# Two transformer blocks on one core: the second half of a layer's output product in three passes of high and low parts

## The chip, the cores and the metric

The kernel runs on one core of one Trainium2 chip. The metric is the device time of one execution in microseconds (us). TensorE (PE in the profile) multiplies; VectorE (DVE) and ScalarE (ACT) do element-wise work; GpSimd (POOL) has little to do here; SyncE (SP) only issues the DMAs that bring the weights from memory. Each engine works through its own list of instructions in order, and semaphores tie the lists together.

## What is computed

A token sequence of 256 (272 with 16 meta tokens in the first block) of width 1024 goes through a first block and then through two hybrid layers. One layer of the second part is, cut to what matters here:

```python
def hybrid_layer(x, ...):
    hn = rms_norm(x, norm1_g)
    proj = jnp.einsum('bsd,df->bsf', hn, w_in)
    ya = mla_mixer(...)              # 8 heads of 64: mixed columns 0 to 511
    yb = stick_breaking_mixer(...)   # 4 heads of 64: mixed columns 512 to 767
    yc = pool_mixer(...)             # 256 mixed columns
    mixed = jnp.concatenate([ya, yb, yc], axis=-1)
    x = x + jnp.einsum('bsm,md->bsd', mixed, w_out)          # the output product
    x = x + hier_moe(rms_norm(x, norm2_g), w_group, b_group, w_expert, b_expert, w_gate, w_up, w_down)
    return x
```

`hier_moe` picks for each token one group of experts and two experts in it; the kernel streams the weights of all 32 experts.

## The kernel before

Everything is kept with features in the 128 partitions and tokens in the free dimension: `hT` is the residual as 8 tiles (index d) of 128 features, `mixT` the mixed columns as 8 tiles of 128 by 256 tokens. All arithmetic is float32. There are two ways of multiplying. A plain float32 product is one matmul in the program, which the profile shows as two records of MATMUL. A split product (`split_mm`, L1274 and after) has both operands as a high part (the value rounded to the short format fp32r, by a copy on ACT) and a low part (the rest, by a subtraction on DVE), and makes three fp32r matmuls: high by high, high by low, low by high; each is one record. The two feed-forward layers of the first block and the last units of each layer's input product use it.

Weights come as a stream of chunks of 1 MB (128 partitions by 2048 floats), one DMA each, issued by SP in `load` (L684), in a fixed order. Before each DMA SP waits until the chunk's place has been freed, and all later DMAs queue behind that wait. Six places are the slots of `ring`. In the expert stage (`moe`) 24 places are used in the order of `moe_slots` (L335): besides the ring these are pieces of `arena`, `G`, `xn`, `sq`, `sm`, `cst`, `mixT` and `hT`, each from the moment at which its old contents are dead (`slot_open`). An expert stage takes 96 chunks in 8 quads of 12, so the first two quads find all their chunks in the 24 places, and each later chunk waits for a place that an earlier quad has used.

The place of the change is in each of the two layers (index l), between the input product and the expert stage. It has three parts:

- The attention loop over 16 units (8 heads for each of two blocks of 128 queries; unit 0 to 7 has 128 keys, unit 8 to 15 has 256). The engines run it with lags, written out by `steps`. PE in step j (L1715 and after): scores of unit j (L1340), one matmul of the output product (`beside`, L1722), the turning of unit j-2's probabilities (L1351, `turn`), up to step 12 a second `beside`, and in each even step the value products of units j-4 and j-3 (L1706, `value_pair`). ACT in step s: save the turned probabilities of unit s-2 (L956, `save_T`), save the output of unit s-4 into `mixT` (L967, `save_o`), exponentials of unit s (L935). DVE in step s: weights of unit s-2 (L2137 reciprocal, L2144 scaling), maximum of unit s (L2121 and L2127).
- The output product is 4 chunks of weights with 2 rows of tiles (f) each, times 8 tiles d of the output: 64 plain products. Its mixed tiles are taken in the order 4, 5, 6, 7, 0, 1, 2, 3, since tiles 0 to 3 come out of the loop. The first 32 products (chunks 0 and 1) are the `beside` matmuls in the loop. The last 32 (chunks 2 and 3) follow the loop in `down` (L1286): chunk 2 row by row, then chunk 3 with both rows for each d, so that output tiles get finished one after another (`y_ready`).
- The residual tail: DVE adds each finished pair of tiles to `hT` (L2402), ACT squares it (L1138), DVE sums the squares (L2393 to L2397), PE makes the token sums and the router's logits (L1754 to L1763), DVE picks the experts, PE gathers their tokens (L1838), and the first quad's gate and up products begin (L1859). They free the first of the 24 places.

## Time and profile before

| | |
|---|---|
| median of 3 runs | 1188.82 us (1187.37 to 1189.06) |
| the profiled execution | 1192.25 us, its span 1190.3 us |
| PE busy | 1116.2 us, 94% of the span |
| DVE, ACT busy | 524.4 us (44%), 427.4 us (36%) |
| bytes read from memory | 321.54 MB, 273 GB/s over the span |
| mean granted TensorE clock | 0.964 |

The profiled execution lies 3.4 us above the median of the runs. All places in time that are given below are microseconds from the start of its span. Layer 0 has its loop at 635.9 to 664.8 us, its output product's second half at 664.8 to 678.8 us and its expert stage up to about 881 us; layer 1 repeats this 302 us later. A busy time of PE is the sum of modelled durations, which overlap; how fast it works is read from the starts of its instructions.

### The profile page before, as it was taken

To read this page: it belongs to the slowest core of one execution; us is meant where nothing else is said; L and a number is where in the kernel's file an instruction comes from. 1 tells how busy PE (TensorE), PEld (TensorE's weight loads), DVE (VectorE), ACT (ScalarE), POOL (GpSimd) and SP (SyncE) were. 2 spreads that over 40 slices of the span, in tenths; PEclk is the share of its full clock that TensorE was granted. 3 is DMA by queue.
4 is the path that set the end of the run, shared out by engine and by line. 5 is a ranking of instruction groups with operands and counts; after the bars stand their busy time and mean duration, and the time that the engine had idled before them with its cause. 6 is when DMAs were issued, how large, how long until landed. Compare 5 with 4: busy or idle time off the path is not lost.

```text
span 1190.3 us, 18825 instructions
## 1 busy us (share of the span) xinstructions
PE 1116.2 (94%) x7912; PEld 867.0 (73%) x7912; DVE 524.4 (44%) x998; ACT 427.4 (36%) x764; POOL 40.7 (3%) x46
## 2 busy tenths in 40 slices
PE   7999999999999999999999998997789999899776
PEld 6999999998568999999997764543359876343321
DVE  5665555885572666555685420110037543011001
ACT  5443345444372543444446420100044543011001
POOL 0000000030010000000030000000004000000000
PEclk9999999999899999999999998998989999899886
DMA  9844442462302545554368699999997879999996
GB/s 362 325 168 170 171 172 105 179 236 107 121 21 96 222 178 180 190 198 178 119 250 347 260 380 419 420 420 421 420 422 289 332 270 363 420 420 420 421 420 273
DMA packets 46058, 323.89 MB, mean 272 GB/s; under 512 B 5401, under 2 KB 5657, under 8 KB 7825
## 3 DMA queue, kind: packets, MB, share of 16 engines
q1 hardware_dynamic: 44736, 318.27, 67.8%
q0 software_dynamic: 688, 3.69, 1.0%
q8 instruction: 66, 1.08, 0.4%
q10 hardware_dynamic: 544, 0.67, 0.2%
q14 instruction: 24, 0.19, 0.0%
HBM read 321.54 MB, written 3.16 MB: 273 GB/s over the span
## 4 chain that ended last, share of the span: by engine, by line
PE 77%; DMA 14%; DVE 5%; ACT 2%; issue 2%; SPq 0%; ACTq 0%; DVEq 0%
PE bank L1276 13%; PE bank L1278 13%; PE bank L1277 13%; DMA ring<-in_stream 9%; PE bank L1859 7%; DMA sq<-in_stream 5%; PE bank L1286 4%; PE bank L1873 3%; PE bank L1838 3%; PE bank L1330 2%; PE bank L1722 2%; PE bank L1340 2%; PE bank L1887 2%; PE bank L1881 1%; PE bank L1657 1%
## 5 line engine op out<-in xcount | busy, mean ns | idle before, releaser
L1276 PE MATMUL bank<-r_hi,w_hi 128*128 128x272 f32 (+1 forms) x928 | 265.8, 286 | 0.0
L1278 PE MATMUL bank<-r_hi,w_lo 128*128 128x272 f32 (+1 forms) x928 | 265.2, 286 | 0.0
L1277 PE MATMUL bank<-r_lo,w_hi 128*128 128x272 f32 (+1 forms) x928 | 264.8, 285 | 0.0
L2011 DVE TENSOR_TENSOR w_lo<-ring,w_hi 128x2048 fp32r<-128x2048 f32 x65 | 148.9, 2292 | 129.7 <-ACT w_hi L888 129.7
L888 ACT ACTIVATE w_hi<-ring 128x2048 fp32r<-128x2048 f32 x65 | 124.5, 1917 | 206.8 <-PE bank L1278 206.8
L1276 PEld LDWEIGHTS bank<-r_hi,w_hi 128*128 128x128 f32 x928 | 175.7, 189 | 0.2
L1278 PEld LDWEIGHTS bank<-r_hi,w_lo 128*128 128x128 f32 x928 | 175.7, 189 | 0.0
L1277 PEld LDWEIGHTS bank<-r_lo,w_hi 128*128 128x128 f32 x928 | 175.4, 189 | 0.1
L2516 DVE TENSOR_TENSOR arena<-arena,bank 128x256 f32<-128x256 f32 x16 | 6.7, 421 | 224.2 <-ACT arena L1174 224.2
L1174 ACT ACTIVATE arena<-bank 128x256 f32<-128x256 f32 x16 | 6.1, 384 | 243.7 <-PE bank L1859 243.7
L1859 PE MATMUL bank<-arena 128*32 128x512 f32 x400 | 57.1, 668 | 18.8 <-DMA arena<-in_stream 10.0
L1838 PEld LDWEIGHTS bank<-rstd,arena 128*128 128x128 f32 x512 | 61.3, 200 | 14.3 <-issue 14.0
L1838 PE MATMUL bank<-rstd,arena 128*128 128x128 f32 x512 | 64.3, 286 | 0.0
L1859 PE MATMUL bank<-ring,arena 128*32 128x512 f32 x320 | 48.8, 695 | 13.9 <-DMA ring<-in_stream 13.9
L1859 PEld LDWEIGHTS bank<-arena 128*32 128x32 f32 x400 | 10.9, 115 | 54.3 <-issue 37.4
L1286 PE MATMUL bank<-mixT,ring 128*128 128x256 f32 x192 | 44.3, 393 | 0.0
L1859 PEld LDWEIGHTS bank<-ring,arena 128*32 128x32 f32 x320 | 9.9, 118 | 45.9 <-DMA ring<-in_stream 27.8
L1286 PEld LDWEIGHTS bank<-mixT,ring 128*128 128x128 f32 x192 | 37.7, 198 | 6.0 <-issue 0.6
L2521 DVE COPY G<-bank 128x512 f32<-128x512 f32 x16 | 11.1, 691 | 69.5 <-PE bank L1873 69.5
L1278 PE MATMUL bank<-hg_hi,ring_r 128*128 128x256 f32 (+1 forms) x136 | 38.6, 284 | 0.0
L1722 PE MATMUL bank<-mixT,ring 128*128 128x256 f32 x128 | 36.9, 382 | 0.0
L1278 PE MATMUL bank<-h_hi,w_lo 128*128 128x272 f32 (+1 forms) x128 | 36.4, 285 | 0.0
(376 smaller groups left out, 1970.7 us busy)
## 6 DMA issues: line engine op xcount, KB each, us to landing
ring<-in_stream SPq DMA_DIRECT2D x149, 1024.0 KB, 5.7
arena<-in_stream SPq DMA_DIRECT2D x72, 1024.0 KB, 18.7
sm<-in_stream SPq DMA_DIRECT2D x16, 1024.0 KB, 23.4
G<-in_stream SPq DMA_DIRECT2D x8, 1024.0 KB, 18.5
w_ukv<-in_stream SPq DMA_DIRECT2D x8, 1024.0 KB, 20.1
xn<-in_stream SPq DMA_DIRECT2D x8, 1024.0 KB, 21.4
sq<-in_stream SPq DMA_DIRECT2D x8, 1024.0 KB, 21.9
cst<-in_stream SPq DMA_DIRECT2D x8, 1024.0 KB, 20.3
```

The source lines that it names most:

```text
L888: copy(w_hi[:, q % 2, :], chunk((A_FFN1, A_FFN2)[f] + q), ACT.Copy).then_inc(S("w_hi_ready"), 1)
L1276: mm(dst, w_high, x_high, start=first, stop=False)
L1277: mm(dst, w_high, x_low, start=False, stop=False)
L1278: return mm(dst, w_low, x_high, start=False, stop=last)
L1286: return mm(y_half(d), w[:, f, P * d:P * d + P], src(2 * c + f), start=c == 0 and f == 0 and d % 2 == 0, stop=c == 3 and f == 1, skip_grou ...
L1330: ins = mm(bank[u - base][:, 0:T2], w[:, k, c0:c0 + P], hg2[:, k, 0:T2], start=(k == 0), stop=(k == KT - 1))
L1340: ins = mm(score_bank(u, g, m)[0:u["nq"], 0:u["L"]], lhs, rhs, start=(j == 0), stop=(j == len(parts) - 1))
L1722: ins = mm(y_half(d), down_view(A_OUT2[l] + c)[:, f, P * d:P * d + P], mixed(2 * c + f), start=n < 8 and d % 2 == 0, stop=False, skip_grou ...
L1838: ins = mm(bank[4 + half][:, P * kk:P * kk + P], x_tm[:, t, P * k:P * k + P], slots[:, s % 2, t, :], start=(t == 0), stop=(t == 1))
L1859: ins = mm(bank[6][CAP * e:CAP * e + CAP, :], xg[:, k, CAP * e:CAP * e + CAP], w[:, e, :], start=(k == 0), stop=(k == KT - 1))
L1873: ins = mm(bank[4 + half][CAP * e:CAP * e + CAP, :], hs[:, f, CAP * e:CAP * e + CAP], w[:, e, :], start=(f == 0), stop=(f == 1))
L2011: V.tensor_tensor(w_lo[:, q % 2, :], chunk((A_FFN1, A_FFN2)[f] + q), w_hi[:, q % 2, :].bitcast(F32), ALU.subtract).then_inc(S("w_lo_ready" ...
```

## The change

The second half of the output product (chunks 2 and 3) is made of split products: 96 fp32r matmuls a layer in the place of 32 plain ones. Their operands have to be split first.

- **Weights.** A half chunk (row f, 128x1024) is copied to its high part by ACT and reduced to its low part by DVE (`split_out` on both). The two halves of chunk 2 are split within the loop: ACT after the exponentials of units 10 and 12, DVE one step later, behind the maximum of units 11 and 13. The high parts of chunk 2 go into chunk 0's ring slot, those of chunk 3 into the first 2048 columns of the arena (`w_hi`), where the queries `qcat` lie, so that the halves of chunk 3 are split behind the loop. The low parts replace the weights in their own slots.
- **Mixed tiles.** For each of tiles 0 to 3, ACT copies the high part (128x256, into a piece of `G`) five steps behind the unit that completes it (`mixed_high`), and DVE makes the low part in place six steps behind it (`mixed_low`).
- **Places.** Chunk 0's ring slot is now free only when chunk 2's products are done. In `moe_slots` it moves from the 15th to the 20th place of the order.

```diff
--- before.py
+++ after.py
@@ -159,7 +159,7 @@
         hg_lo = xn_r
         sq = sb("sq", [P, 10, T1])
         rstd = sb("rstd", [P, 2, T1])
-        mixT = sb("mixT", [P, KT, T1])
+        mixT, mixT_r = both("mixT", [P, KT, T1])
         G, G_r = both("G", [P, 8, GX])
         cst = sb("cst", [P, C_ALL])
         gn = sb("gn", [P, G_ALL])
@@ -335,7 +335,7 @@
         def moe_slots(ring_slot):
 
             order = ([S_AR + 1, ring_slot[4], S_AR, ring_slot[5], S_G, S_UKV, S_XN, S_SQ, S_SM] + [S_AR + j for j in range(2, 7)]
-                     + [ring_slot[0], S_CST, S_AR + 7, S_AR + 8] + ring_slot[1:4] + [S_MIX, S_ROOT, S_HT])
+                     + [S_CST, S_AR + 7, S_AR + 8] + [ring_slot[j] for j in (1, 2, 0, 3)] + [S_MIX, S_ROOT, S_HT])
             assert sorted(order) == list(range(NS2))
             return order
 
@@ -388,10 +388,14 @@
         rows_lo = G_r[:, :, :].rearrange("p a b -> p (a b)")[:, 0:CH].rearrange("p (k n) -> p k n", k=KT)
 
         def layer_split(l, p):
-            return SPLIT_AT[1] + 3 * FC + 4 * l + p - 2 + 1
+            return SPLIT_AT[1] + 3 * FC + 8 * l + p - 2 + 1
+
+        def out_split(l, c, f):
+            return layer_split(l, 6 + 2 * (c - 2) + f)
 
         def layer_hi(p):
             return (in_hi[0], w_ukv1_r[:, :])[p % 2].rearrange("p (k n) -> p k n", k=KT)
+        mix_hi = G_r[:, :, :].rearrange("p a b -> p (a b)")[:, CH:CH + D].rearrange("p (k n) -> p k n", k=4)
         FFN_ROOT = [1, 5]
         GAINED = 4
 
@@ -584,6 +588,7 @@
             else:
                 if n == MOE_AT[l]:
                     turn, around = 0, slot_of[A_IN2[l]:A_IN2[l] + NS]
+                    last[slot_of[A_OUT2[l]]] = freed[A_OUT2[l] + 2]
                 order = moe_slots(around)
                 if n - MOE_AT[l] >= QUADS * QCH - NS2:
                     order = last_slots(order)
@@ -625,6 +630,10 @@
 
         def layer_lo(l, p):
             return ring_r[:, slot_of[A_IN2[l] + p], :].rearrange("p (k n) -> p k n", k=KT)
+
+        def out_parts(l, c, f):
+            hi = ring_r[:, slot_of[A_OUT2[l]], :] if c == 2 else w_hi[:, 0, :]
+            return tuple(v[:, D * f:D * f + D] for v in (hi, ring_r[:, slot_of[A_OUT2[l] + c], :]))
 
         def in_cols(p):
             return P if p == 2 else 256
@@ -877,6 +886,12 @@
                     act.wait_ge(S("proj_ready"), U1 + U2 * l + 2 * p - 2)
                 copy(layer_hi(p), up_view(A_IN2[l] + p), ACT.Copy).then_inc(S("w_hi_ready"), 1)
 
+            def split_out(l, c, f):
+                loaded(act, A_OUT2[l] + c)
+                name, v = freed[A_OUT2[l]] if c == 2 else ("scores_ready", SEG_M[l][1])
+                act.wait_ge(S(name), v)
+                copy(out_parts(l, c, f)[0], down_view(A_OUT2[l] + c)[:, f, :], ACT.Copy).then_inc(S("w_hi_ready"), 1)
+
             def square_unit(u, dst, src):
                 first_saved(act, u)
                 copy(dst, src, ACT.Square).then_inc(S("square_saved"), 1)
@@ -1131,7 +1146,20 @@
                             nc.scalar.activation(mixT[:, 6 + t, 0:T2], bank[3][:, T2 * t:T2 * t + T2], ACT.Copy,
                                                  scale=gain(G_PS + 2 * l + t)).then_inc(S("pool_saved"), 1)
 
-                steps(SEG_M[l], (save_T, 2), (save_o, 4), (exps, 0), (save_pool, 0))
+                def out_weights(g):
+                    if g - SEG_M[l][0] in (10, 12):
+                        split_out(l, 2, (g - SEG_M[l][0] - 10) // 2)
+
+                def mixed_high(g):
+                    n = g - SEG_M[l][0]
+                    if n >= MH and n % 2 == 1:
+                        k = (n - MH) // 2
+                        act.wait_ge(S("o_saved"), g + 1)
+                        copy(mix_hi[:, k, :], mixT[:, k, 0:T2], ACT.Copy).then_inc(S("mix_hi_ready"), 1)
+
+                steps(SEG_M[l], (save_T, 2), (save_o, 4), (exps, 0), (save_pool, 0), (out_weights, 0), (mixed_high, 5))
+                for f in range(2):
+                    split_out(l, 3, f)
                 link(copy(rs[:, 0, :], sums[:, 0, :], ACT.Sqrt))
                 for d in range(KT):
                     act.wait_ge(S("residual_ready"), 8 * (3 + 2 * l) + d + 1)
@@ -1742,7 +1770,24 @@
                     n += count
                     if j >= 4 and j % 2 == 0:
                         value_pair(g - 4)
-                down(A_OUT2[l], 2, 4, mixed, lambda k: [("o_saved", SEG_M[l][1] - 7 + 2 * (k - 4) + 1)])
+                def out_part(c, f, d, end=False):
+                    hi, lo = (v[:, P * d:P * d + P] for v in out_parts(l, c, f))
+                    x_hi, x_lo = mix_hi[:, 2 * (c - 2) + f, :], mixT_r[:, 2 * (c - 2) + f, 0:T2]
+                    mm(y_half(d), hi, x_hi, start=False, stop=False, skip_group_check=True)
+                    mm(y_half(d), hi, x_lo, start=False, stop=False, skip_group_check=True)
+                    return mm(y_half(d), lo, x_hi, start=False, stop=end, skip_group_check=True)
+
+                for c in (2, 3):
+                    for f in range(2):
+                        pe.wait_ge(S("w_lo_ready"), out_split(l, c, f))
+                        pe.wait_ge(S("mix_lo_ready"), 4 * l + 2 * (c - 2) + f + 1)
+                        for d in range(KT if c == 2 else 0):
+                            ins = out_part(c, f, d)
+                    if c == 2:
+                        ins.then_inc(S("down_used"), 1)
+                for d in range(KT):
+                    out_part(3, 0, d)
+                    out_part(3, 1, d, end=True).then_inc(S("y_ready"), 1)
                 last = l == LAYERS - 1
                 x_bank = 0 if last else 4
                 log_bank, place_bank, load_bank = (bank[4], bank[5], bank[7]) if last else (bank[0], bank[1], bank[0])
@@ -1997,6 +2042,11 @@
                 dve.wait_ge(S("w_hi_ready"), layer_split(l, p))
                 V.tensor_tensor(layer_lo(l, p), up_view(A_IN2[l] + p), layer_hi(p).bitcast(F32), ALU.subtract
                                 ).then_inc(S("w_lo_ready"), 1)
+
+            def split_out(l, c, f):
+                hi, lo = out_parts(l, c, f)
+                dve.wait_ge(S("w_hi_ready"), out_split(l, c, f))
+                V.tensor_tensor(lo, down_view(A_OUT2[l] + c)[:, f, :], hi.bitcast(F32), ALU.subtract).then_inc(S("w_lo_ready"), 1)
 
             def scale_unit(l, u):
                 dve.wait_ge(S("proj_ready"), U1 + U2 * l + u + 1)
@@ -2383,7 +2433,21 @@
                     src = bank[(15 + n) % 4].rearrange("p (a n) -> p a n", a=2)
                     link(V.tensor_copy(kcat[0:64, 4 * n:4 * n + 4:2, :], src[0:64]))
                     V.tensor_copy(kcat[0:64, 4 * n + 1:4 * n + 4:2, :], src[64:128]).then_inc(S("unit_read"), 1)
-                steps(SEG_M[l], (weights, 2), (maxes, 0))
+                def out_weights(g):
+                    if g - SEG_M[l][0] in (10, 12):
+                        split_out(l, 2, (g - SEG_M[l][0] - 10) // 2)
+
+                def mixed_low(g):
+                    n = g - SEG_M[l][0]
+                    if n >= MH and n % 2 == 1:
+                        k = (n - MH) // 2
+                        dve.wait_ge(S("mix_hi_ready"), 4 * l + k + 1)
+                        V.tensor_tensor(mixT_r[:, k, 0:T2], mixT[:, k, 0:T2], mix_hi[:, k, :].bitcast(F32), ALU.subtract
+                                        ).then_inc(S("mix_lo_ready"), 1)
+
+                steps(SEG_M[l], (weights, 2), (maxes, 0), (out_weights, 1), (mixed_low, 6))
+                for f in range(2):
+                    split_out(l, 3, f)
 
                 def add_squares(d):
                     if d == 0:
```

Within the loop this changes the lists of ACT and DVE. In the rows, a name such as `arena<-bank` is written<-read. ACT in layer 1, from the exponentials of unit 9 to those of unit 11, before (L956 is `save_T`, L967 `save_o`, L935 the exponentials):

```order
L935 ACTIVATE arena,sums<-arena,nmx 128x256 [waits max_ready]
L956 ACTIVATE arena<-bank 128x256 [waits o_ready,aT_ready]
L967 ACTIVATE mixT<-bank 64x128 [waits o_ready]
L935 ACTIVATE arena,sums<-arena,nmx 128x256 [waits max_ready]
L956 ACTIVATE arena<-bank 128x256 [waits o_ready,aT_ready]
L967 ACTIVATE mixT<-bank 64x128 [waits o_ready]
L935 ACTIVATE arena,sums<-arena,nmx 128x256 [waits max_ready]
```

The same place now (L971, L982 and L950 are the same three lines, L893 is the high copy of half a chunk):

```order
L950 ACTIVATE arena,sums<-arena,nmx 128x256 [waits max_ready]
L971 ACTIVATE arena<-bank 128x256 [waits o_ready,aT_ready]
L982 ACTIVATE mixT<-bank 64x128 [waits o_ready]
L950 ACTIVATE arena,sums<-arena,nmx 128x256 [waits max_ready]
L893 ACTIVATE ring_r<-ring 128x1024 [waits down_used,slot2_loaded]
L971 ACTIVATE arena<-bank 128x256 [waits o_ready,aT_ready]
L982 ACTIVATE mixT<-bank 64x128 [waits o_ready]
L950 ACTIVATE arena,sums<-arena,nmx 128x256 [waits max_ready]
```

The high copy stands between the exponentials of unit 10 and the saving of unit 9's turned probabilities. DVE in layer 0, from the maximum of unit 11 to that of unit 12, before:

```order
L2121 ISA arena,mx<-bank,cst 128x256 [waits scores_ready,probs_ready]
L2121 ISA mx 128x1
L2127 TENSOR_SCALAR nmx<-mx 128x1 [waits scores_taken]
L2137 RECIPROCAL rs<-sums 128x1 [waits aT_ready,exps_ready]
L2144 TENSOR_SCALAR arena<-arena,rs 128x256 [waits dve_chain]
L2121 ISA arena,mx<-bank,cst 128x256 [waits scores_ready,probs_ready]
```

And now (L2171, L2177, L2187 and L2194 are the same lines, L2049 is the low part of half a chunk):

```order
L2171 ISA arena,mx<-bank,cst 128x256 [waits scores_ready,probs_ready]
L2171 ISA mx 128x1
L2177 TENSOR_SCALAR nmx<-mx 128x1 [waits scores_taken]
L2049 TENSOR_TENSOR ring_r<-ring,ring_r 128x1024 [waits w_hi_ready]
L2187 RECIPROCAL rs<-sums 128x1 [waits aT_ready,exps_ready]
L2194 TENSOR_SCALAR arena<-arena,rs 128x256 [waits dve_chain]
L2171 ISA arena,mx<-bank,cst 128x256 [waits scores_ready,probs_ready]
```

The low part, with its wait for ACT's high copy, stands ahead of the weights of unit 10. The same insertion stands once more two steps later, ahead of the weights of unit 12.

## Rows read from the trace of the kernel before

**Rows 1.** The page, section 4: the chain that ended last, by engine
```profile
PE 77%; DMA 14%; DVE 5%; ACT 2%; issue 2%; SPq 0%; ACTq 0%; DVEq 0%
```

**Rows 2.** The chain of waits: start us, us, what; product, first residual, token sums; product of layer 1
```profile
664.88 8.84 PE bank L1286 x40
673.83 0.44 DVE hT L2402
...
681.06 0.61 PE bank L1758 x4
...
967.15 8.85 PE bank L1286 x40
```

**Rows 3.** Chain, then timeline of PE: plain 128x256 records, then fp32r ones (L1276, L1277)
```profile
585.73 6.91 PE bank L1330 x32
...
593.33 0.28 PE L1277 MATMUL bank<-G_r,in_hi 128*128 128x256 f32 x1
...
598.89 0.28 PE L1276 MATMUL bank<-xn_r,w_ukv_r 128*128 128x256 f32 x1
```

**Rows 4.** Timeline of ACT in the loop: start us, us, ..., [idle before <-releaser]
```profile
653.72 0.19 ACT L935 ACTIVATION_READ_ACCUMULATOR arena<-arena,nmx 128x1 f32 x1
...
656.70 0.38 ACT L956 ACTIVATE arena<-bank 128x256 f32<-128x256 f32 x1 [1.28 <-PE bank L1706]
...
657.54 0.19 ACT L935 ACTIVATION_READ_ACCUMULATOR arena<-arena,nmx 128x1 f32 x1
...
660.49 0.19 ACT L935 ACTIVATION_READ_ACCUMULATOR arena<-arena,nmx 128x1 f32 x1
...
663.40 0.38 ACT L956 ACTIVATE arena<-bank 128x256 f32<-128x256 f32 x1 [0.25 <-PE bank L1351]
```

**Rows 5.** Timeline of DVE in the loop: maximum of unit 13, weights of unit 14
```profile
657.39 0.42 DVE L2121 CUSTOM_DVE_ANT_0 arena<-bank,cst 128x256 f32<-128x256 f32 x1 [1.20 <-PE bank L1340]
...
660.89 0.16 DVE L2137 RECIPROCAL rs<-sums 128x1 f32<-128x1 f32 x1
661.08 0.35 DVE L2144 TENSOR_SCALAR arena<-arena,rs 128x256 f32<-128x256 f32 x1
```

**Rows 6.** Timeline of PE in the loop: turns of units 10, 12, 14; last value pair
```profile
655.21 0.38 PE L1351 MATMUL bank<-cst,arena 128*128 128x128 f32 x2
...
658.59 0.39 PE L1351 MATMUL bank<-cst,arena 128*128 128x128 f32 x2
...
661.49 0.44 PE L1351 MATMUL bank<-cst,arena 128*128 128x128 f32 x2 [0.21 <-DVE arena L2144]
...
664.23 0.66 PE L1706 MATMUL bank<-arena 128*64 128x128 f32 x8 [0.43 <-ACT mixT L967]
```

**Rows 7.** Groups by line and form, 570 to 900 us: busy us, mean ns
```profile
L839 ACT ACTIVATE xn_r<-arena 128x1024 fp32r<-128x1024 f32 x4 | 4.0, 1042 | 0.0
...
L1998 DVE TENSOR_TENSOR ring_r<-ring,w_ukv_r 128x2048 fp32r<-128x2048 f32 x3 | 8.4, 2799 | 0.1
...
L1992 DVE TENSOR_TENSOR G_r<-arena,xn_r 128x1024 fp32r<-128x1024 f32 x4 | 4.7, 1218 | 0.0
```

**Rows 8.** Stretches: length, busy us of PE, PEld, DVE, ACT, POOL; granted clock, DMA share, GB/s
```profile
690.00:693.00 3.00, 3.00 (x29) 1.36 (x31) 0.69 (x1) 1.76 (x3) 0.00 (x0) 1.00 0.37 101
...
714.00:717.00 3.00, 0.00 (x0) 0.00 (x0) 0.00 (x0) 0.00 (x0) 0.00 (x0) 0.80 1.01 412
717.00:720.00 3.00, 2.74 (x16) 0.90 (x20) 0.00 (x0) 0.00 (x0) 0.00 (x0) 0.50 1.03 426
```

**Rows 9.** Timeline of SP: issue of the chunk for `cst`, and of the first refill
```profile
660.80 0.33 SPq L684 DMA_DIRECT2D cst<-in_stream  x1
...
691.98 0.33 SPq L684 DMA_DIRECT2D arena<-in_stream  x1
```

**Rows 10.** The chain of waits in the expert stage: 64 records of gate and up
```profile
690.92 7.00 PE bank L1859 x64
...
717.26 9.71 PE bank L1859 x64
```

## The prediction

> **What bounds the kernel now.** I read the chain that ended last first. PE carries 77% of it and DMA 14% [rows 1], so the question at any place is which of the two sets the end there. Around the change the answer is plain. The second half of the output product lies on the chain: it starts at 664.88 us, and its first 40 records take 8.84 us before DVE can take the first residual tile at 673.83 [rows 2]. Layer 1 shows 8.85 us for the same 40 [rows 2]. From there the chain runs through DVE and ACT (adding, squaring, summing, choosing experts) to the gather and the first quad.
>
> Then I looked at what follows, because a DMA-bound stage could swallow a gain or a loss. In the expert stage the DMA engines are full (share 1.01 to 1.03 at 714 to 720 us, 412 to 426 GB/s), while PE does not work at all for a while [rows 8]. But that stream is full only from the moment at which the first places come free: at 690 to 693 us the DMA share is 0.37 [rows 8], and the first refill is issued at 691.98 [rows 9], just after the first quad's products begin at 690.92 [rows 10]. All 24 places are loaded by then, and 72 chunks are still to come, at 1.05 MB by 0.42 MB per us = 2.5 us each, about 180 us that no engine can shorten. So the expert stage ends a fixed time after its first quad begins. What the change does to the arrival at 690.92 passes to the end one for one, and the same once more in layer 1. The share of PE's busy time says nothing here; the arrival at the first quad is everything.
>
> Within the loop the rows show how tight the engines are coupled. PE has practically no idle time up to step 14; its first wait for DVE is 0.21 us at 661.49 and the last 0.43 us at 664.23 [rows 6]. ACT and DVE have idle stretches of 1.28 and 1.20 us [rows 4, 5], but they lie in front of a wait for PE, not where the change puts its work.
>
> **Part 1, the product itself.** Plain records follow each other at 6.91 / 32 = 0.216 us, and a plain product is two of them, 0.432 us. From 593.33 to 598.89 there are 47 steps between fp32r matmuls of the same form (128x256, each with weights of its own), 0.118 us each [rows 3]; a split product is three, 0.355 us. What counts is the time to the first pair of finished output tiles: 16 products of chunk 2 and 4 of chunk 3. Before 20 x 0.432 = 8.64 us, now 20 x 0.355 = 7.10 us, a gain of 1.54 us a layer. The last 12 products get faster as well, but DVE and ACT need 0.9 us for each output tile (8 of them from 673.83 to the token sums at 681.06 [rows 2]), against 0.86 us of PE before and 0.71 us now: the tail is theirs, and that gain is worth nothing.
>
> The rows make a split product 0.82 of a plain one. The Trainium skill (FP8 and Floating Point Precision, TensorE Precision Notes) counts true FP32 as four passes, high and low by high and low. By that three passes would be 0.75 of a plain product, 0.324 us, and the gain would be 2.16 us; the trace shows less, and I do not use it.
>
> **Part 2, the weights' splits in the loop.** This is where I expect the price. ACT's high copy of 1024 columns takes 1.04 us and DVE's low part 1.22 us [rows 7], and both stand in lists that are worked in order. Follow layer 0 (all times as in the profile of before, plus the shift so far).
>
> First split. ACT's exponentials of unit 10 end at 653.72 + 0.19 = 653.91 [rows 4]. The high copy runs from 653.95 to 654.99. DVE waits for it and makes the low part until 656.24. Only then come the weights of unit 10, whose two instructions take 0.54 us (660.89 to 661.43 [rows 5]): ready at 656.80, and PE turns unit 10 at 656.86 in the place of 655.21 [rows 6]. PE stands at that turn, with nothing else to do, since its list too is in order: **1.65 us**. ACT's copy alone would have been hidden by its 1.28 us of idle time before 656.70; it is the sum of both, in series, ahead of the weights, that isn't.
>
> Second split. ACT's step 12 starts with a save at 656.70, which waits for PE's value pair, so it shifts to 658.35; the exponentials of unit 12 end at 657.54 + 0.19 + 1.65 = 659.38. High copy to 660.44, low part to 661.70, weights of unit 12 to 662.25, turn at 662.31 in the place of 658.59 [rows 4, 6]: 3.72 in all, so **2.07 us** more. It is more than the first time because PE gives these steps only one product of its own, so less time lies between the exponentials and the turn.
>
> **Part 3, the mixed tiles.** The high copy (128x256) takes about 0.42 us on ACT, its subtraction about 0.43 us on DVE, by the nearest rows: the same engines' ops of 256 columns [rows 4, 5] show 0.38 and 0.42. The first stands behind the exponentials of unit 14 (660.49 + 0.19 + 3.72 = 664.40) and ahead of the weights of unit 14 on DVE: 664.40 + 0.44 + 0.43 = 665.27, weights to 665.81, turn of unit 14 at 665.87 in the place of 661.49 [rows 6]: 4.38 in all, **0.66 us** more. The second stands on ACT between the save of unit 12's output and the save of unit 15's probabilities (663.40 in rows 4), which had 0.25 us of idle time: about **0.2 us** more for the last value pair. The two others lie behind the loop. The loop ends 1.65 + 2.07 + 0.66 + 0.2 = 4.6 us late.
>
> **Part 4, the splits behind the loop.** PE begins chunk 2 at 664.8 + 4.6 = 669.4 and needs 48 x 0.118 = 5.7 us for it, to 675.1. Meanwhile ACT has the last two saves (0.27 us each), two high copies of 0.42 and two of 1.04, from 669.5 to 673.0, and DVE's last low part ends about 674.5. It is covered, but by 0.6 us only. Where the low part takes half of 2.80 us, as L1998 showed in another place [rows 7], each is 0.2 us longer and the cover is 0.2 us; so nothing is charged, and 0.5 us is kept for the upper end. ACT's table load for the square root follows at 673.0 and is over before the first residual.
>
> **Part 5, the places.** Chunk 0's slot was reloaded in the loop; now ten loads (25 us) remain from the one for `cst`, issued at 660.80 before [rows 9] and about 664.5 now. If they ran without a gap they would land at 689.5; the last of them cannot be issued before the tokens are turned, about 687, so the first round is complete by about 692. The refill starts at 691.98 + 3.1 = 695. Hidden, with some 3 us of cover; in the layer without any stall it would still be about 1 us. In the last quad of layer 0 the slot is freed four chunks later, while the chunks ahead of it in the queue still load: no cost.
>
> **The sum.** 4.6 - 1.5 = 3.1 us late at the first quad, in each layer, 6.2 us in all. From the profiled execution that is 1192.25 + 6.2 = 1198.4; it lies 3.4 us above the median, so the median should be 1188.8 + 6.2 = **1195.0 us**. Bounds of this case: if the mixed tiles' copies cost nothing, since ACT and DVE have caught up by then, 2 x (3.7 - 1.6) = 4.2 us, 1193.0; if the low parts take 1.4 us and the cover of chunk 3 fails by 0.5 us, 2 x (5.0 + 0.5 - 1.5) = 8 us, 1196.8, with 0.7 us of scatter 1197.5.
>
> **Rivals.**
> *The splits vanish in idle time, faster.* ACT is idle 1.28 us and DVE 1.20 us in every second step [rows 4, 5]. If DVE's list let the weights of units 10 and 12 be ready before the turn needs them, no stall would remain, and the price would be nothing or 0.3 us of the mixed tiles: 2 x (1.5 - 0.3) = 2.4 us to 3.1 us faster, 1185.7 to 1186.4. Against it: the weights stand behind the low part, and PE's turn of unit 10 had a margin of only 0.5 us (weights ready at about 654.7). Chance 0.09.
> *The stalls are half as long, no change.* PE's waits at steps 16 to 18 (0.21 and 0.43 us [rows 6]) and the latencies there could absorb part of a shift that has come earlier, since then ACT and DVE have caught up. If a layer's stalls came to 1.5 to 2.7 us, the sum would be within 2.4 us of before, 1188.8 to 1191.2. Against it: the extra work of the mixed tiles sits in just these steps. Chance 0.11.
> *The clock falls, much slower.* Where PE stood still from about 713 to 717 us, the granted clock was 0.80 and then 0.50 [rows 8], the lower of the two levels, 1.2 GHz, and 64 records took 9.71 in the place of 7.00 us [rows 10]. If a wait of 2 us were enough, each of the four stalls could cost up to 2.7 us more: two of them 5.4 us, 1200.4. Against it: the idle time before that fall was about twice as long. The Trainium skill (TensorE: Matmul & The Clock Gate, HAM oscillation — how this bites in real kernels) warns of gaps between bursts of matmuls in the same way; for gaps as short as these the trace shows no fall. Chance 0.05.
> *The product gains nothing.* If the three passes took 0.432 us (the high and low operands come from `G`, `mixT` and two ring slots, not from the places of the rows), the sum would be 9.2 us, 1198.0. Chance 0.03.
>
> **How the numbers follow.** My own case has 0.72. A measurement of this kernel tells about 0.2% from no change, 2.4 us, so slower means over 1191.2: 0.72 + 0.05 + 0.03 = 0.80. Within 0.2%: 0.11. Faster: 0.09. The range for 8 in 10 takes in my case's bounds, the upper part of the half-long stalls and the product without gain: 1190.0 to 1198.5.
>
> **What would show each step.** In the profile of the changed kernel: 60 fp32r records in about 7.1 us between the start of the product and the first residual (under 7.3 right, near 8.6 the fourth rival); PE idle before the turn of units 10 and 12 by 1.4 to 2.3 us each, released by DVE's L2194, with DVE's L2049 just before it (idle under 0.5 us: the first rival); the loop 4 to 5 us longer, 33 or 34 in the place of 29 us; no wait of PE for chunk 3's low part; granted clock 1.00 through the loop; the first refill about 3 us later, and the DMA share over 1.00 from there on. I would be wrong as a whole if the expert stage did not keep its length from the first quad on.

## The result, and the profile after

The changed kernel takes 1195.11 us (median of 6 runs, 1194.32 to 1199.02), the kernel before 1188.50 us beside it (6 runs, 1187.37 to 1189.38): 6.6 us more. The ratio of the two is 1.0058, with a 95% interval of 1.0044 to 1.0072, which is 6.9 us (5.2 to 8.6) slower. A repeat gave 1.0051 (1.0034 to 1.0068). The profiled execution took 1195.35 us, its span is 1193.2 us.

The page, section 4, of the changed kernel: the chain that ended last, by engine:
```profile
PE 76%; DMA 14%; DVE 5%; ACT 3%; issue 2%; SPq 0%; ACTq 0%; DVEq 0%
```
PE has a point less than in [rows 1] and ACT one more. The shares say little; the chain in order of time tells what happened. Here it is through layer 0 of the changed kernel (start us, us, engine and what, records):
```profile
634.60 0.88 PE bank L1750 x4
...
652.13 0.96 ACT ring_r L893
653.11 0.04 DVE ring_r L2049
653.14 1.11 issue
654.25 0.17 DVE rs L2187
...
657.43 0.95 ACT ring_r L893
...
658.44 1.11 issue
...
677.90 0.43 DVE hT L2466
...
691.21 7.00 PE bank L1904 x64
```
What is new on the chain is twice the same sequence: ACT's high copy (L893, 0.96 us to the next instruction), DVE's low part (the two pieces 0.04 and "issue" 1.11: the chain does not name the subtraction itself), and then only the weights of the unit (L2187, L2194). I take as the loop's start its first record of the output product, 0.46 us behind the first scores in both kernels. It is at 634.60 and the first quad's products begin at 691.21, 56.61 us; before it was 636.38 to 690.92, 54.54 us [rows 10]. Layer 1 takes 57.11 us in the place of 54.83 by the same two records.

PE's timeline in the changed kernel shows the same from the waiting side (turns of units 10, 12, 14, last value pair, product; in brackets the idle time before and who ended it):
```profile
654.85 0.44 PE L1379 MATMUL bank<-cst,arena 128*128 128x128 f32 x2 [1.27 <-DVE arena L2194]
...
660.15 0.44 PE L1379 MATMUL bank<-cst,arena 128*128 128x128 f32 x2 [1.70 <-DVE arena L2194]
...
663.58 0.44 PE L1379 MATMUL bank<-cst,arena 128*128 128x128 f32 x2 [0.69 <-DVE arena L2194]
...
666.31 0.66 PE L1734 MATMUL bank<-arena 128*64 128x128 f32 x8 [0.43 <-ACT mixT L982]
666.90 0.39 PE L1776 MATMUL bank<-G_r,ring_r 128*128 128x256 f32 x1
```
The first two of these turns had no idle time before and the third 0.21 us [rows 6]. The last 0.43 us is the old one [rows 6].

DVE and ACT in the same stretch of the changed kernel (timeline; the bracket is again idle time and its releaser):
```profile
652.03 1.05 ACT L893 ACTIVATE ring_r<-ring 128x1024 fp32r<-128x1024 f32 x1
...
653.11 1.22 DVE L2049 TENSOR_TENSOR ring_r<-ring,ring_r 128x1024 fp32r<-128x1024 f32 x1 [0.70 <-ACT ring_r L893]
...
654.25 0.15 DVE L2187 RECIPROCAL rs<-sums 128x1 f32<-128x1 f32 x1
654.44 0.35 DVE L2194 TENSOR_SCALAR arena<-arena,rs 128x256 f32<-128x256 f32 x1
...
662.63 0.43 DVE L2445 TENSOR_TENSOR mixT_r<-mixT,G_r 128x256 fp32r<-128x256 f32 x1
```
DVE stands idle for 0.70 us for ACT's copy, subtracts for 1.22 us, and the weights, for which PE waits, stand behind both.

The rest as far as it answers to the rows of before. The product (60 fp32r records to the first finished pair):
```profile
672.72 0.28 PE L1776 MATMUL bank<-G_r,w_hi 128*128 128x256 f32 x1
...
674.34 0.76 DVE L2466 SCALAR_TENSOR_TENSOR hT<-bank,hT 128x256 f32<-128x256 f32 x2 [2.71 <-PE bank L1778]
```
From the product's start in the chain, 666.97, to the first residual tile, 674.34, it is 7.37 us; before 664.88 to 673.83, 8.95 us [rows 2]. The tail from there to the token sums takes 7.24 us (674.34 to 681.58), before 7.23 [rows 2]. Chunk 3's first product (672.72) has no wait in front of it; its low parts were ready at 671.63, 1.1 us earlier:
```profile
668.20 2.00 ACT L893 ACTIVATE w_hi<-ring 128x1024 fp32r<-128x1024 f32 x2
...
669.27 2.36 DVE L2049 TENSOR_TENSOR ring_r<-ring,w_hi 128x1024 fp32r<-128x1024 f32 x2 [0.52 <-ACT w_hi L893]
```
SP's issues of the load for `cst` and of the first refill, answering to [rows 9]:
```profile
662.42 0.33 SPq L693 DMA_DIRECT2D cst<-in_stream  x1
...
692.26 0.33 SPq L693 DMA_DIRECT2D arena<-in_stream  x1
```
Counted from the loop's start the first refill comes at 57.66 us where it was 55.60, later by 2.06 us, just as much as the first quad (2.07). The stretches (length; busy us of PE, PEld, DVE, ACT, POOL; granted clock, DMA share, GB/s) answer to [rows 8]:
```profile
690.00:693.00 3.00, 3.00 (x31) 1.64 (x34) 1.20 (x4) 2.05 (x4) 0.00 (x0) 1.00 0.47 194
693.00:696.00 3.00, 3.00 (x36) 0.91 (x30) 0.00 (x0) 0.00 (x0) 0.00 (x0) 1.00 0.86 300
696.00:699.00 3.00, 3.00 (x31) 1.26 (x23) 0.31 (x1) 0.38 (x1) 0.00 (x0) 1.00 1.00 421
```
The DMA engines fill up as the refills begin; from 700 to 880 us their share is 1.01.

For all that follows I use four stages, cut by rows of the chain: the loop's start (as above) to the first quad (layer 0), from there to the loop of layer 1, the same two in layer 1, the last ending at the last record of the chain. In us:

| kernel | loop to quad, layer 0 | to next loop | loop to quad, layer 1 | to the end |
|---|---|---|---|---|
| before | 54.54 | 247.72 | 54.83 | 193.63 |
| changed | 56.61 | 247.21 | 57.11 | 194.51 |

### The profile page after: what moved, and what is told of

Its sections match the earlier page's. It is cut to its first block, busy times and chain, and to the rows that moved or that the text cites. A ratio compares the mean times of both kernels' runs of the same rounds, so it can differ in the third digit from the quotient of the medians.

```text
span 1193.2 us, 18997 instructions
## 1 busy us (share of the span) xinstructions
PE 1110.8 (93%) x7976; PEld 862.1 (72%) x7976; DVE 536.9 (45%) x1014; ACT 436.5 (37%) x780; POOL 40.7 (3%) x46
## 4 chain that ended last, share of the span: by engine, by line
PE 76%; DMA 14%; DVE 5%; ACT 3%; issue 2%; SPq 0%; ACTq 0%; DVEq 0%
PE bank L1304 13%; PE bank L1306 13%; PE bank L1305 13%; PE bank L1904 6%; DMA ring<-in_stream 5%; PE bank L1883 4%; PE bank L1918 3%; DMA sq<-in_stream 2%; PE bank L1314 2%; PE bank L1358 2%; DMA arena<-in_stream 2%; DMA mixT<-in_stream 2%; DMA hT<-in_stream 2%; PE bank L1750 2%; PE bank L1926 2%
## 5 line engine op out<-in xcount | busy, mean ns | idle before, releaser
L1750 PE MATMUL bank<-mixT,ring 128*128 128x256 f32 x128 | 36.9, 382 | 0.0
L1304 PE MATMUL bank<-h_hi,w_hi 128*128 128x272 f32 (+1 forms) x128 | 36.4, 285 | 0.0
L1305 PE MATMUL bank<-h_lo,w_hi 128*128 128x272 f32 (+1 forms) x128 | 36.4, 285 | 0.0
```

The costliest lines, as they stand in the source:

```text
L1304: mm(dst, w_high, x_high, start=first, stop=False)
L1305: mm(dst, w_high, x_low, start=False, stop=False)
L1750: ins = mm(y_half(d), down_view(A_OUT2[l] + c)[:, f, P * d:P * d + P], mixed(2 * c + f), start=n < 8 and d % 2 == 0, stop=False, skip_grou ...
```

## The experiments

**Theory:** the loss is the in-series placing of high copy and low part ahead of a unit's weights, and the product itself is a gain. **Rivals:** the gain is smaller than I read; the stalls hide another cost (mixed tiles, places, clock); a difference between two executions and not between kernels.

### The kernel before, again

No edit. 

> The kernel before, unchanged, as a kernel of its own: a ratio of 1.000 to itself, and a second profile of it. Both theories of the 2 us that lie between the difference of the medians (6.6 us) and the sum of the shifts in the two traces (about 2.1 + 2.3 us at the first quads) meet here. Theory A: the first profile of before contained a disturbance of 2 to 3 us outside the changed place (the 64 plain records at 356.7 us took 16.0 us there and 14.0 us in the changed kernel), so this profile's own time lies at 1188 to 1190 us and those records take 14.0 us. Theory B: it is a property of the kernel before, and the records take 16.0 us again.

Measured: 1190.17 us (1187.41 to 1192.40) beside 1189.21, ratio 1.000 (0.9979 to 1.0022). Stages 54.55, 247.85, 54.82, 193.75: the loop repeats to 0.01 us. The expert stages vary more: in eleven of the thirteen profiles (all but the two of the last two experiments below, the long stall and the place) both together take 439.6 to 443.9 us.

What stood open was that everything ahead of the loop was 1.8 us shorter in the changed kernel's profile. It comes from one block, the first of the first feed-forward, here in the chain of before:
```profile
356.74 16.04 PE bank L1286 x64
```
and of the changed kernel:
```profile
356.97 14.01 PE bank L1314 x64
```
Of the thirteen profiles seven show 15.8 to 16.2 us (both of before, two of the changed kernel among them) and six 14.01 (two of the changed kernel): it belongs to an execution, not to a kernel. So the half of the expectation that took it for a property of the kernel falls, and so does the other, which expected 14.0 us here and found 16.20.

The granted clock tells what it is. Stretches of before, then one of the changed kernel at the same work (columns as before; the granted clock is the third last number):
```profile
351.20:354.00 2.80, 2.79 (x12) 2.15 (x13) 2.60 (x9) 0.95 (x4) 0.00 (x0) 1.00 0.03 6
354.00:357.00 3.00, 3.00 (x12) 2.25 (x11) 1.16 (x6) 0.88 (x4) 0.00 (x0) 0.50 0.00 0
357.00:360.60 3.60, 3.60 (x9) 2.86 (x9) 0.53 (x2) 0.55 (x3) 0.00 (x0) 0.50 0.00 0
...
355.00:358.00 3.00, 3.00 (x18) 2.47 (x17) 1.76 (x8) 1.43 (x5) 0.00 (x0) 1.00 0.03 5
```
The clock stood at its lower level, 1.2 GHz, for between 6 and 7 us, and the block began within that time. All seven profiles with the long block show this, none of the six with 14.01 us does. The longest wait that PE's timeline of before shows between 320 us and the block is one of 0.57 us, ended at 351.21. All thirteen profiles have it, and the seven falls begin 2.6 to 2.9 us behind its end; that this wait brings them is not shown. So the kernel before has a fall of the clock too, with no wait near as long as the stalls of 1.27 and 1.70 us ahead of it.

### The low parts behind the weights

```
-steps(SEG_M[l], (weights, 2), (maxes, 0), (out_weights, 1), (mixed_low, 6))
+steps(SEG_M[l], (weights, 2), (out_weights, 2), (maxes, 0), (mixed_low, 6))
```
DVE does the weights of units 10 and 12 first and the low part after them. 

> The changed kernel with one difference: DVE makes the low parts of chunk 2's halves behind the weights of units 10 and 12, no longer ahead of them (ACT's list stays). My theory (the price is the position in DVE's list, ahead of the weights that PE's turn waits for): the stall at the turn of unit 10 goes to 0, that of unit 12 too, a stall of 0.8 us appears at the turn of unit 13, 0.6 us at that of unit 14 remain, the loop ends 1.4 to 1.7 us late in the place of 3.9, so 2.2 to 2.5 us a layer are won back: 4.4 to 5 us under the changed kernel, about 1190 us, within 0.2% of before. Rival (the work itself, 2.3 us of ACT and DVE for each half, is too much for the loop wherever it stands): no more than 0.5 us of difference to the changed kernel, 1195 us.

Measured: 1188.82 us, ratio 1.000 (0.9986 to 1.0014); stages 53.78, 249.64, 54.28, 192.35. The stalls of 1.27 and 1.70 us are gone. The wait of 0.8 us that was expected at the turn of unit 13 did not come, and the loop ends 1.03 us late (expected 1.4 to 1.7). PE's timeline shows what was late instead:
```profile
658.14 0.66 PE L1734 MATMUL bank<-arena 128*64 128x128 f32 x8 [0.41 <-ACT mixT L982]
...
661.27 0.44 PE L1379 MATMUL bank<-cst,arena 128*128 128x128 f32 x2 [0.58 <-DVE arena L2194]
...
664.01 0.66 PE L1734 MATMUL bank<-arena 128*64 128x128 f32 x8 [0.43 <-ACT mixT L982]
```
One entry moved in one list gives back 2.83 us per layer in the traces (56.61 to 53.78, 57.11 to 54.28). The first quad is then 0.76 and 0.55 us ahead of before. The work is the same on every engine; so it isn't the splits' amount that costs, but where they stand in DVE's list. The timed medians show about 1 us less gain than the first quads.

### The price alone: all splits, plain product

```
-    mm(y_half(d), hi, x_hi, ...)
-    mm(y_half(d), hi, x_lo, ...)
-    return mm(y_half(d), lo, x_hi, ...)
+    return mm(y_half(d), down_view(A_OUT2[l] + c)[:, f, P * d:P * d + P], mixed(2 * c + f), ...)
```
The low parts are written over the high ones, so that weights and mixed tiles stay whole. 

> The changed kernel with all its splits in their places, but with the second half of the output product as 32 plain products, as before; the low parts are written over the high parts, so that weights and mixed tiles stay whole. It measures the price of the splits alone. My theory: each layer's loop ends 3.9 us late and nothing is won in the product, 2 x 3.9 = 7.8 us over before, 1196.3 us; the difference to the changed kernel is then the gain of the three passes, 1.6 us a layer. Rival (the three passes win nothing, as in the fourth rival): the same time as the changed kernel, within 1 us.

Measured: 1197.89 us, ratio 1.0075 (1.0060 to 1.0089); stages 58.17, 247.21, 58.68, 193.26. PE waits as in the changed kernel, 1.27, 1.70, 0.69 and 0.43 us. In its chain chunk 2 and half of chunk 3 stand as
```profile
667.34 10.57 PE bank L1775 x48
```
48 plain records at 0.220 us. The difference to the changed kernel at the first quad is the gain of the three passes alone: 58.17 - 56.61 = 1.56 us, 58.68 - 57.11 = 1.57 us. The price alone is 3.63 and 3.85 us. Both halves of the theory have their number. The median lies 1.6 us above the 1196.3 expected: it is 8.7 us over before where the traces show 7.5.

### All splits earlier

```
-if g - SEG_M[l][0] in (10, 12):
-    split_out(l, 2, (g - SEG_M[l][0] - 10) // 2)
+if g - SEG_M[l][0] in (7, 9):
+    split_out(l, 2, (g - SEG_M[l][0] - 7) // 2)
-... (maxes, 0), (out_weights, 1), (mixed_low, 6))
+... (out_weights, 2), (mixed_low, 6), (maxes, 0))
-... (out_weights, 0), (mixed_high, 5))
+... (out_weights, 0), (mixed_high, 4))
```
ACT copies after the exponentials of units 7 and 9 (the condition stands on both engines), DVE's low parts go behind the weights, the mixed tiles' copies one step earlier on ACT. 

> The changed kernel with its work in the loop moved into idle time: ACT's high copies of chunk 2 behind the exponentials of units 7 and 9 (ahead of ACT's long wait of each even step), DVE's low parts one stage later and ahead of the maximum (where DVE waits for the scores), ACT's first mixed copy one step earlier, its low part ahead of the maximum of unit 15. My theory: no stall of more than 0.3 us is left, the loop ends 0 to 0.4 us late, and the 1.6 us of the product remain: 2.4 to 3.1 us a kernel faster than before, about 1186 us, ratio 0.9975 to 0.998. Rival (ACT and DVE have no room at all in the loop): over 1190 us.

Measured: 1185.20 us, ratio 0.9976 (0.9962 to 0.9991); stages 52.72, 247.45, 53.21, 192.23. In PE's timeline the one wait left in the loop is the old one:
```profile
662.06 0.66 PE L1734 MATMUL bank<-arena 128*64 128x128 f32 x8 [0.43 <-ACT mixT L982]
```
The first quad is 1.82 and 1.62 us ahead of before: the whole gain of the product (1.56 and 1.57), and in layer 0 the 0.23 us of the router that the part on the forecast tells of. The same instructions as in the changed kernel, in another order, beat both kernels.

### That version, again

No further edit. 

> The version with the three kinds of splits put earlier in the lists, a second time and with more rounds. Theory (the stalls were the loss and the product the gain): first quads 52.7 and 53.2 us after the loop's start, no wait in the loop but the old one of 0.43 us, no fall of the clock, ratio to the kernel before 0.997 to 0.998 (1185.0 to 1186.5 us). If the first result was luck, the ratio is 0.999 to 1.001.

Measured: 1185.31 us (1182.00 to 1188.18), ratio 0.9968 (0.9956 to 0.9980), beside 1188.92. Stages 52.72, 247.27, 53.21, 192.34. By the ratios of the first measurement and this one it is 2.9 and 3.8 us faster than before; the first quads give 3.4.

### Weights early, mixed tiles as they were

```
 the three changes above, but
-... (out_weights, 2), (mixed_low, 6), (maxes, 0))
+... (out_weights, 2), (maxes, 0), (mixed_low, 6))
 and (mixed_high, 5) as in the changed kernel
```


> The fastest kernel so far with its mixed tiles' copies put back to where the changed kernel has them; only the weights' splits are moved. It measures the mixed tiles' price alone. Theory by the trace of the changed kernel (the third shift, at the turn of unit 14, was 0.5 us): the loop ends 0.4 to 0.7 us late, and the first quad begins 54.5 - 1.8 + 0.5 = 53.2 to 53.4 us after the loop's start (52.7 with the copies moved too, 54.5 before). Rival (the 0.5 us only came about behind two stalls): 52.7 us.

A single run, 1190.54 us, too little to compare whole times; stages 53.23, 248.73, 53.74, 195.18. PE waits for the mixed tile's split in one place only:
```profile
659.97 0.44 PE L1379 MATMUL bank<-cst,arena 128*128 128x128 f32 x2 [0.69 <-DVE arena L2194]
```
Against the version with all splits early the mixed tiles cost 0.51 and 0.53 us a layer.

### The changed kernel, again

No edit. 

> The changed kernel once more, unchanged, beside the kernel before on the same chip. The traces show its first quads 2.1 and 2.3 us later, counted from the start of each layer's loop, 4.4 us in all; the first measurement was 1.0058, 6.9 us (5.2 to 8.6). Theory A: the loop is the whole of it, and the rest came from the rate of the weights' stream, which differs from run to run by up to 1% (416 to 421 GB/s in the traces so far): ratio 1.002 to 1.005, 1192 to 1195 us. Theory B: the change costs something more in the expert stages: ratio 1.005 to 1.007, and stages from the first quad to the next layer's loop longer than 247.9 us.

Measured: 1195.84 us (1190.90 to 1199.32) beside 1189.89, ratio 1.0051 (1.0034 to 1.0068). Stages 56.61, 248.66, 57.89, 192.29. The ratio fits both theories of the expectation. The second wanted longer expert stages; layer 0's is longer (248.66), but both together take 440.95 us, less than the 441.35 of before. All stalls repeat to 0.01 us, but layer 1 takes 0.78 us more than in the first profile. Its timeline of PE shows why:
```profile
966.06 0.44 PE L1379 MATMUL bank<-cst,arena 128*128 128x128 f32 x2 [1.70 <-DVE arena L2194]
966.43 0.66 PE L1734 MATMUL bank<-arena 128*64 128x128 f32 x8
967.01 1.21 PE L1368 MATMUL bank<-arena 128*128 128x256 f32 x2
968.02 1.06 PE L1750 MATMUL bank<-mixT,ring 128*128 128x256 f32 x2
```
and the stretches (columns as before) say what happened:
```profile
966.00:967.00 1.00, 0.94 (x10) 0.62 (x10) 0.90 (x6) 0.00 (x0) 0.00 (x0) 1.00 0.00 0
967.00:969.00 2.00, 2.00 (x7) 1.51 (x6) 0.74 (x5) 1.34 (x5) 0.00 (x0) 0.51 0.00 0
969.00:970.60 1.60, 1.60 (x7) 1.04 (x5) 0.75 (x3) 1.01 (x3) 0.00 (x0) 0.54 0.47 82
970.60:973.00 2.40, 1.97 (x17) 1.30 (x16) 0.94 (x3) 1.70 (x7) 0.00 (x0) 1.00 0.91 382
```
A microsecond after the second stall the clock goes to its lower level, 1.2 GHz, for some 3.6 us. Two records of 128x256 take 1.06 us in the place of 0.60. This is the rival of the falling clock, which the first profile didn't show at all.

### Two more profiles of the changed kernel, and one with longer stalls

> The changed kernel unaltered, for two more layers of its loop in a profile. Stalls of 1.26, 1.70, 0.69 and 0.43 us in both. Theory A (the clock falls now and then behind the second stall): first quads 56.6 and 57.1 us after the loop's start where it doesn't, about 0.8 us more where it does, with a granted clock near 0.5 for 3 to 4 us; one layer of the four seen so far had it. Theory B (what was seen once has another cause than the stalls): it doesn't come back behind them, and the time that a layer's loop takes is 56.6 to 57.1 us always.

> As the run before: two more layers of the changed kernel's loop. Together with it the rate at which the clock falls behind the second stall is known from eight layers: by Theory A one to four of them show it.

The two runs took 1194.96 and 1194.37 us. First quads after 56.63 and 57.90 us in one, 56.62 and 57.14 in the other. The 57.90 has the fall in the same place:
```profile
965.05 0.44 PE L1379 MATMUL bank<-cst,arena 128*128 128x128 f32 x2 [1.70 <-DVE arena L2194]
...
966.01 1.12 PE L1368 MATMUL bank<-arena 128*128 128x256 f32 x2
```
Then the stalls were made longer, by two more high copies ahead of the real one whose result nobody uses:
```
+if c == 2:
+    for _ in range(2):
+        link(copy(out_parts(l, c, f)[0], down_view(A_OUT2[l] + c)[:, f, :], ACT.Copy))
 copy(out_parts(l, c, f)[0], down_view(A_OUT2[l] + c)[:, f, :], ACT.Copy).then_inc(S("w_hi_ready"), 1)
```


> The changed kernel, but ACT makes the high copy of each half of chunk 2 three times in the place of once (the first two for nothing), so that PE stands at the turns of units 10 and 12 about 2.2 us longer each: 3.4 and 3.9 us in the place of 1.26 and 1.70. What it is for: in one profile of the changed kernel (the repeat, layer 1) the granted clock was 0.51 for 3.6 us just after the second stall, and the first quad came 0.8 us later than in layer 0; in the other profile it was not. Theory A (the stalls themselves are the price, and the clock falls only now and then behind them): first quads at 61.0 and 61.5 us after the loop's start, 4.4 more in each layer, granted clock 1.00 in the loop in most layers, 1195.5 + 8.8 = 1204.3 us. Theory B (a longer stall brings the clock down each time): a stretch of 3 to 4 us at a clock near 0.5 behind one of the two stalls in each layer, 0.8 to 2.7 us more each, 62 to 66 us per layer, 1206 to 1212 us.

Measured: 1206.38 us (1204.44 to 1209.72), ratio 1.0142 (1.0127 to 1.0156). Stalls of 3.44 and 3.08 us in layer 0, and behind each of them the clock was down. PE's timeline of layer 0:
```profile
657.16 0.44 PE L1382 MATMUL bank<-cst,arena 128*128 128x128 f32 x2 [3.44 <-DVE arena L2197]
657.44 0.92 PE L1753 MATMUL bank<-mixT,ring 128*128 128x256 f32 x2
...
665.43 0.69 PE L1382 MATMUL bank<-cst,arena 128*128 128x128 f32 x2 [3.08 <-DVE arena L2197]
```
Its first records after a stall are long at once (0.92 in the place of 0.60 us). The stretches behind the two stalls:
```profile
657.20:660.00 2.80, 2.80 (x14) 1.74 (x15) 0.97 (x5) 0.50 (x3) 0.00 (x0) 0.57 0.00 0
...
665.40:667.00 1.60, 1.57 (x10) 1.01 (x10) 1.03 (x5) 0.00 (x0) 0.00 (x0) 0.50 0.00 0
667.00:669.50 2.50, 2.50 (x9) 1.94 (x8) 0.99 (x5) 1.33 (x5) 0.00 (x0) 0.50 0.03 7
```
The granted clock is 0.57 and 0.50. The first quad comes 63.53 us after the loop's start in layer 0, 62.99 in layer 1, where 61.0 and 61.5 had been expected from the stalls alone. That leaves some 2.5 and 1.5 us for the clock; this is an estimate, since a slower PE also reaches the second stall later and waits less there (3.08 us, expected 3.9). Theory B of this run holds: the longer stalls brought the clock down in both layers, the time lies in its range. Its first quads sum to 8.99 + 8.16 = 17.2 us over before; the medians differ by 17.5.

With the stall of 1.70 us the clock fell in 2 of 12 layers (four profiles of the changed kernel and those of the price alone and of the place), at 0.8 us each; with stalls of 3 us and more in 2 of 2; in the 12 layers of the six profiles without a stall over 0.7 us in the loop (two of before, four of versions with moved splits), never. This does not make the length of the stall the rule: ahead of the loop the clock fell in 7 of 13 profiles with no wait over 0.57 us in front of it.

### Chunk 0's place put back

```
-+ [S_CST, S_AR + 7, S_AR + 8] + [ring_slot[j] for j in (1, 2, 0, 3)] +
++ [ring_slot[0], S_CST, S_AR + 7, S_AR + 8] + ring_slot[1:4] +
```
The slot is refilled at its old turn, though the split parts hold it longer now. 

> The changed kernel with chunk 0's ring slot at its old, 15th place in the order of the loads. SP then waits for the end of chunk 2's products (about 672.7 us) ahead of the loads for cst, two arena pieces and the rest of the ring: ten loads (25 us) run from there without a gap to about 698, and the refill, asked for at 692, follows behind. My theory (an expert stage ends a fixed time after its stream of weights is full): the first quad begins as in the changed kernel, but the stage ends about 5 us later in each layer, 10 us over the changed kernel, 1203 to 1206 us. Rival (the stage has reserves in the DMA stream, its end is set by PE): within 2 us of the changed kernel.

Measured: 1204.27 us, ratio 1.0132 (1.0110 to 1.0154); stages 56.62, 253.49, 57.12, 198.20. SP's timeline in this version:
```profile
670.86 0.33 SPq L693 DMA_DIRECT2D ring<-in_stream  x1
671.27 0.38 SPq L693 DMA_DIRECT2D cst<-in_stream  x1
```
The load for `cst` goes out at 671.27, because the one ahead of it in the queue waits for its slot. Counted from the loop's start (632.54 here) that is 38.73 us, 10.9 later than in the changed kernel (27.82). The first quad doesn't notice (56.62), but the expert stages are longer by 6.3 and 3.7 us than in the changed kernel's first profile, and the median by 8.4 us than the changed kernel's beside it. So the first quad doesn't tell everything: a stream that starts late is not caught up. The new places of the change are needed.

## Why the forecast came out, step by step

All counted from the loop's start, layer 0, in us:

| step | forecast | measured |
|---|---|---|
| turn of unit 10 late | 1.65 | 1.42 |
| turn of unit 12, further | 2.07 | 1.92 |
| turn of unit 14, further | 0.66 | 0.53 |
| last value pair, further | 0.2 | 0.0 |
| loop late | 4.6 | 3.87 |
| gain of the product | 1.54 | 1.58 |
| router, won back | 0 | 0.23 |
| first quad late | 3.1 | 2.07 |

**What bounds it** held. The four profiles of the changed kernel have both expert stages together at 440.8 to 441.7 us, the two of before at 441.4 and 441.6: the shift at the first quad passes to the end, to within 1 us. Over the eleven profiles named above the two stages scatter by 4.3 us, so this is all that can be said. The place experiment shows the condition, that the first 24 chunks are on their way in time.

**Part 1** held to 0.04 us. The rows of fp32r matmuls in another place gave the spacing, and the spacing was the same here. The experiment with the plain product gives the same gain, 1.56 and 1.57 us. That the last 12 products win nothing held too: the tail took 7.24 us after 7.23. The Trainium skill (FP8 and Floating Point Precision, TensorE Precision Notes) counts true FP32 as four passes; the estimate from it, three of four passes at equal cost, was a gain of 2.16 us, and the trace shows less.

**Part 2** had the mechanism right: L2049 just before L2187 and L2194, released by ACT's copy, PE waiting for L2194. It is 0.23 and 0.15 us too large in its two terms, because I set instruction behind instruction by their full durations. The chain has the high copy at 0.96 us where the timeline has 1.05, since the copy begins 0.1 us before the instruction ahead of it ends; and from the start of the low part (653.11) to that of the next instruction (654.25) it is 1.14 where its duration is 1.22. Over two instructions in series this is 0.17 us.

**Part 3**: 0.53 instead of 0.66, for the same reason; the experiment with the weights early gives 0.51 and 0.53 by itself. The second term, 0.2 us for the last value pair, never came. From the turn of unit 14 to the last value pair it is 2.73 us, before 2.74 [rows 6]: ACT's copy of 0.41 us fitted into the 0.25 us of idle time, since it began (665.13) 0.1 us before the save ahead of it ended (665.23) and the save behind it began (665.49) before it had ended. This is the overlap again, and it does not need the two long stalls: it is 2.74 us too in the versions that lack them and keep ACT's mixed copies as they were.

**Part 4** held, with 1.1 us of cover in the place of 0.6.

**Part 5** held: the places cost nothing, with the refill just behind the first quad. My time for it (695) was too late by the amount by which all else was too late.

**The sum** is where I was off inside a right total. Per layer the trace shows 2.07 and 2.28 us, not 3.1: 4.35 us in both. The gap is the mis-sized terms of parts 2 and 3 (0.7) and, in layer 0, 0.23 us that the router won back, which I had not looked for: its two DVE instructions behind the logits (L2418, now L2482) take 0.65 us together in layer 0 of both profiles of before, 0.42 in layer 1, and 0.42 in both layers of every other profile, the one with the plain product among them. The code there is the same; the cause stays open. The timed medians differ by 6.6 and 6.0 us all the same. Of the gap to 4.35 the clock falling in the loop explains at most 0.4 us a run (0.8 us in 2 of 8 layers of the changed kernel, two layers a run), and the end does not show even that: in the two profiles with this fall the last stage took 192.3 us, in the other two 193.7 and 194.5. The rest, 1 to 2 us, stays open. The fall ahead of the loop costs 2 us where it comes, so its rate in the timed runs, which no run here shows, could move a median by as much. The intervals begin at 5.2 and 4.0 us, so for the second measurement nothing need be missing. The profiles show no other stage that is longer, and both profiles of before took more than the median of their kernel (1192.25 and 1191.06 against 1188.50 to 1189.89), so a comparison of profiles understates the difference. That my total fits the medians better than my terms fit the trace is partly luck.

**The rivals.** *Splits vanish in idle time*: false as the lists are written, true once they are reordered (the version with all splits early), and then worth a little more than I had given it, 1185.2 and 1185.3 us against 1185.7 to 1186.4. *Half as long*: false; the loop was 3.87 us late, not 1.5 to 2.7. *The clock falls*: I gave it 0.05 and wrote that the trace shows no fall for gaps as short as these. That was misread: the trace I had before me shows one at 354.0 us, behind a wait of 0.57 us. In the loop it comes in 2 of 12 layers, for 0.8 us and not 2.7; with stalls of 3 us it comes in both layers seen. The Trainium skill (TensorE: Matmul & The Clock Gate, HAM oscillation — how this bites in real kernels) warns of gaps between bursts of matmuls, in an example where PE waits longer than 1.70 us each time. The runs agree for the long stalls, and show falls behind shorter waits as well, in some executions only. *The product gains nothing*: false, 1.56 us.

## What to carry to other kernels

Where each engine works an ordered list, extra work is priced by what stands behind it and who waits for that, not by how much idle time the engine has: the same splits cost 3.6 to 3.9 us a layer ahead of the wrong instruction and nothing where ACT begins them three steps earlier and DVE does them behind the weights. Put work that nobody needs soon behind the instruction that somebody waits for, and, if it has two halves on two engines, start the first half steps ahead, so that the second engine never stands waiting for it. What a faster product brings is only known once its preparation has been placed.

## What the runs showed of the hardware

- Consecutive instructions of one engine overlap: ACT's copy of 1024 columns has 1.05 us and the chain moves on after 0.96; DVE's subtraction has 1.22 us and the next instruction starts after 1.14. In these two places a sum of durations is too large by about 0.1 us for each step. It is not so everywhere: the reciprocal behind the subtraction ends at 654.40 and the scaling starts at 654.44.
- After a stall of 1.70 us the granted clock fell to about 0.5 in 2 of 12 layers, after stalls of 3.4 and 3.1 us in both layers seen. After the shorter stall the fall came about 1 us after PE had begun to work again, after the longer ones at once. The same program shows it in one execution and not in the next.
- No long wait is needed for a fall: ahead of the loop the clock went to 0.50 for 6 to 7 us in 7 of 13 profiles, 2.6 to 2.9 us behind the end of a wait of 0.57 us that all thirteen have. A block of 64 records takes 15.8 to 16.2 us there in the place of 14.0. Two profiles can so differ by 2 us ahead of the place of the change; stages are to be counted from a record close to it.
- The loops repeat to 0.03 us where the clock holds. The expert stages of the changed kernel scatter by 1.5 us in layer 0 and 2.2 us in layer 1, and not by the rate of the stream: from 8 to 188 us behind the first quad of layer 0 it is 420 or 421 GB/s in all thirteen profiles. Layer 1's stage goes with the clock: with the place experiment and the long stall left aside, it takes 192.2 to 192.4 us in the five profiles whose granted clock from 150 to 192 us behind the first quad was 0.88 to 0.92, and 193.3 to 195.2 us in the six with 0.79 to 0.84. Which is cause and which effect is not shown.
